# One weight unit's low part on GpSimd, and another order of VectorE's additions and low parts behind the pooled products

## The reference, cut to what matters

```python
x = x + _pool_mixer(h, pool_prev[i], pool_mask, w_pool[i], pool_scale[i])
h = _rmsnorm(x, g_ffn[i])
x = x + _swiglu(h, w1_dense[i // 2], w3_dense[i // 2], w2_dense[i // 2])
# _pool_mixer: y = einsum('btgc,gce->btge', diff, w_pool) * scale
# _rmsnorm:    y = x * rsqrt(mean(x * x) + EPS) * g
# _swiglu:     (silu(h @ w1) * (h @ w3)) @ w2
```

## Time and profile before

| | us |
|---|---|
| median of 3 runs | 1482.81 (1482.11 to 1485.51) |
| the profiled execution's own time | 1484.52 |
| its span in the profile | 1482.7 |
| TensorE busy | 1454.6 (98%) |
| VectorE busy | 1199.4 (81%) |
| ScalarE busy | 1019.6 (69%) |
| GpSimd busy | 35.8 (2%) |

### The profile page before, as it was taken

How to read it: one execution, slowest core, us unless ns; L and a number is a source line. 1 busy time by engine, 2 the same in 40 slices (tenths; PEclk the granted TensorE clock), 3 DMA queues, 4 the chain that set the end, 5 groups by cost and what they waited for, 6 DMA issues and landing times.

```text
span 1482.7 us, 23159 instructions
## 1 busy us (share of the span) xinstructions
PE 1454.6 (98%) x7980; PEld 1278.9 (86%) x7980; DVE 1199.4 (81%) x1441; ACT 1019.6 (69%) x1292; POOL 35.8 (2%) x66
## 2 busy tenths in 40 slices
PE   7999999999999999999999999999999999999997
PEld 7999999999988888888888888888888888888787
DVE  6745545458875899998999999999989999899897
ACT  5433333356786777777877877777787777787776
POOL 2000000000000000000000000000000000000000
PEclk9999999999999999999999999999999999999999
DMA  9434443435413999999999999999999999999951
GB/s 355 175 142 154 144 155 143 152 140 192 164 44 121 359 368 388 381 385 390 360 387 381 352 410 373 363 403 379 373 391 379 385 375 381 388 361 399 378 198 36
DMA packets 65827, 437.69 MB, mean 295 GB/s; under 512 B 8643, under 2 KB 10307, under 8 KB 14704
## 3 DMA queue, kind: packets, MB, share of 16 engines
q1 hardware_dynamic: 62592, 426.87, 74.6%
q0 software_dynamic: 2768, 9.89, 2.6%
q10 hardware_dynamic: 416, 0.26, 0.1%
HBM read 428.22 MB, written 8.77 MB: 295 GB/s over the span
## 4 chain that ended last, share of the span: by engine, by line
PE 93%; DVE 4%; ACT 1%; DMA 1%; issue 1%; SPq 0%; DVEq 0%; ACTq 0%; POOLq 0%
PE PS L742 90%; PE PS L1158 2%; DMA s_G<-in_x_rows 1%; PE PS L1114 0%; DVE s_Al L1254 0%; DVE s_Sl L1241 0%; DMA s_G<-rows_dram,s_ix 0%; DVE s_xT L1320 0%; ACT s_hT L452 0%; DVE s_st L1495 0%; ACT s_Sh L440 0%; PE PS L1064 0%; PE PS L1191 0%; ACT s_sq L452 0%; DVE s_Al L1246 0%
## 5 line engine op out<-in xcount | busy, mean ns | idle before, releaser
L1241 DVE TENSOR_TENSOR s_Sl<-s_raw,s_Sh 128x1024 fp32r<-128x1024 f32 x798 | 937.3, 1221 | 131.2 <-ACT s_Sh L440 130.2
L440 ACT ACTIVATE s_Sh<-s_raw 128x1024 fp32r<-128x1024 f32 x798 | 799.4, 1052 | 215.1 <-PE PS L742 208.5
L742 PE MATMUL PS<-s_Sh,s_Ah 128*128 128x512 f32 x1344 | 529.9, 394 | 0.0
L742 PE MATMUL PS<-s_Sh,s_Al 128*128 128x512 f32 x1344 | 524.1, 390 | 0.0
L742 PE MATMUL PS<-s_Sl,s_Ah 128*128 128x512 f32 x1344 | 523.6, 390 | 0.0
L742 PE MATMUL PS<-s_Ah,s_Sh 128*128 128x320 f32 x1008 | 314.0, 312 | 3.2 <-DVE s_Sl L1241 1.2
L742 PE MATMUL PS<-s_Ah,s_Sl 128*128 128x320 f32 x1008 | 311.8, 309 | 0.0
L742 PE MATMUL PS<-s_Al,s_Sh 128*128 128x320 f32 x1008 | 311.8, 309 | 0.0
L742 PEld LDWEIGHTS PS<-s_Sh,s_Al 128*128 128x128 f32 x1344 | 252.4, 188 | 53.2
L742 PEld LDWEIGHTS PS<-s_Sh,s_Ah 128*128 128x128 f32 x1344 | 252.7, 188 | 50.8
L742 PEld LDWEIGHTS PS<-s_Sl,s_Ah 128*128 128x128 f32 x1344 | 252.9, 188 | 50.6
(11 more groups left out here) (216 smaller groups left out, 586.1 us busy)
## 6 DMA issues: line engine op xcount, KB each, us to landing
s_raw<-in_w_moe SPq DMA_DIRECT2D x336, 1024.0 KB, 6.5
s_raw<-in_w_trunk SPq DMA_DIRECT2D x63, 1024.0 KB, 4.8
y_dram<-s_G POOLq DMA_DIRECT2D x3, 512.0 KB, 4.0
s_xT<-in_xT SPq DMA_DIRECT2D x2, 640.0 KB, 15.3
s_G<-in_x_rows SPq DMA_DIRECT2D x2, 512.0 KB, 5.6
rows_dram<-s_G SPq DMA_DIRECT2D x4, 256.0 KB, 2.0
s_G<-y_dram SPq DMA_DIRECT2D x2, 512.0 KB, 7.5
out_y<-s_G SPq DMA_DIRECT2D x2, 512.0 KB, 3.0
```

Of the source, the lines that this page charges most:

```text
L440: nc.scalar.activation(Sh[:, q % NSPL, o:o + UNIT // 2], raw[:, q % NRAW, o:o + UNIT // 2], ACT.Copy).then_inc(hi_ready, 1)
L742: return nc.tensor.matmul(out, w, m, start=start, stop=stop, **kw)
L1241: last = nc.vector.tensor_tensor(Sl[:, q % NSPL, o:o + UNIT // 2], raw[:, q % NRAW, o:o + UNIT // 2], Sh[:, q % NSPL, o:o + UNIT // 2].bit ...
```

## The change

GpSimd makes the low part of unit 2, behind unit 1's, in the same two halves; VectorE no longer does. VectorE adds chunks 0 and 1 ahead of `lo(1)`, makes the low parts of chunks 0 and 1 behind it, then adds chunks 2 and 3 and makes theirs. `lo(3)` moves from behind the sum tree to ahead of it, behind a wait for the third low part. ScalarE makes the high part of unit 3 between chunks 3 and 4 in place of behind the squares, and the squares follow the last high part. TensorE's and SP's streams are not changed.

```diff
--- before.py
+++ after.py
@@ -381,6 +381,12 @@
             pool.wait_ge(hrows_ready, 3)
             pool.dma_start(A["pool_prompt"], hrows[P - HIST:P, 1, :]).then_inc(pool_stored, 16)
             pool.dma_start(A["pool_sample"], hrows[TS - HIST:TS, 2, :]).then_inc(pool_stored, 16)
+            pool.wait_ge(lo_ready, 2)
+            for half in range(2):
+                o = half * (UNIT // 2)
+                pool.wait_ge(hi_ready, 5 + half)
+                last = pool.tensor_tensor(Sl[:, 2, o:o + UNIT // 2], raw[:, 2, o:o + UNIT // 2], Sh[:, 2, o:o + UNIT // 2].bitcast(F32), ALU.subtract)
+            last.then_inc(lo_ready, 1)
             pool.wait_ge(unit_done, Q_PROJ + 1)
             pool.memset(xrow, 0.0).then_inc(consts, 1)
             pool.wait_ge(consts, NCONST + 2)
@@ -486,11 +492,12 @@
                 act.wait_ge(band_done, c + 1)
                 nc.scalar.activation(Ah3[:, c, :], PS[:, c, 0:T], ACT.Copy).then_inc(hh_ready, 1)
             hi(1)
+            act.wait_ge(vec_loaded, 16)
             hi(2)
-            act.wait_ge(vec_loaded, 16)
-            high_g(1, G_FFN0, 1)
+            high_g(1, G_FFN0, 1, 0, 4)
+            hi(3)
+            high_g(1, G_FFN0, 1, 4, KC)
             squares(1, 0, KC)
-            hi(3)
             root(1)
 
             def silu(r, b):
@@ -1304,13 +1311,15 @@
             for c in range(KC):
                 v.wait_ge(hh_ready, c + 1)
                 low(Al3[:, c, :], PS[:, c, 0:T], Ah3[:, c, :], hl_ready)
-            lo(1)
             v.wait_ge(vec_loaded, 16)
             for c in range(KC):
+                if c == 2:
+                    lo(1)
+                    low_g(1, G_FFN0, 0)
+                    low_g(1, G_FFN0, 1)
                 if c == 4:
-                    for d in range(4):
-                        low_g(1, G_FFN0, d)
-                    lo(2)
+                    low_g(1, G_FFN0, 2)
+                    low_g(1, G_FFN0, 3)
                 if c % 4 == 0:
                     v.wait_ge(x_loaded[c // 4], 16)
                 if c < KC - 1:
@@ -1322,8 +1331,9 @@
                 if c > 4:
                     low_g(1, G_FFN0, c - 1)
             low_g(1, G_FFN0, KC - 1)
+            v.wait_ge(lo_ready, 3)
+            lo(3)
             tree(1)
-            lo(3)
             norm(1)
             link(nc.vector.memset(rsc[:, :], 1.0))
             v.wait_ge(consts, 4)
```

## The result

| | us | runs |
|---|---|---|
| before, on the same chips | 1483.14 (1481.68 to 1486.20) | 22 |
| the change | 1486.58 (1484.05 to 1490.35) | 22 |
| ratio | 1.0024, 95% interval 1.0018 to 1.0030 | |
| the profiled execution of the change | 1485.56 (span 1483.8) | 1 |

The change is slower, by 3.4 us between the medians. That is 0.24% (0.18 to 0.30), just above the 0.2% (3.0 us) that the prediction set as the smallest difference to be told from none, and inside its range.

What follows compares the result with a forecast made beforehand. TensorE, busy 98% of the span, was taken to bound the kernel. Chunk 2 3.72 us late, less 1.24 us gained at unit 3, gave 2.5 us slower: 1485.3 us, range 1481.1 to 1487.4.

Steps and rivals of the forecast that it cites:

- The forecast's mechanism: GpSimd's two halves each hold a VectorE activation low part, so TensorE starts chunk 2 3.72 us late; chance 0.40.
- C: Rival: VectorE held twice and TensorE's clock falls in the waits; 3.7 us slower, 1486.5 us, chance 0.13.
- the likeliest, without the fall: Forecast case: VectorE's low parts held twice, TensorE's clock unchanged; 2.5 us slower, 1485.3 us, chance 0.40.
- The fall: TensorE's granted clock dropping to 1.2 GHz around its waits before chunk 2; at most 1.7 us, put at 1.2.
- The wait for unit 3: TensorE's idle time behind the sum of squares, for weight unit 3's low part; 1.24 us, expected to go entirely.
- A, no hold: Rival: GpSimd's and VectorE's subtractions run side by side, only 1.24 us gained; 1481.6 us, chance 0.25.
- B, held once: Rival: VectorE's first two low parts both go between GpSimd's halves; 0.9 us slower, 1483.7 us, chance 0.22.
- The places where I had found cover: TensorE reaches the square sum at 45.0, ready near 44; unit 3's scaled gate has 0.7 us of cover.
- no change: Outcome for the whole kernel: a difference of under 0.2% (3.0 us) from before; chance 0.67.

Runs made afterwards that it cites:

- e4: The change with GpSimd's low part of unit 2 in four instructions of 512 columns instead of two of 1024; 1484.26 us, ratio 1.0003.
- e6: The kernel before with only GpSimd's making of unit 2's low part added; 1484.01 us, ratio 1.0004.
- e7: The change with GpSimd's two subtractions replaced by four fills of nearly the same total length; 1481.94 us, ratio 0.9987.
- e8: The change with GpSimd also waiting until the low parts of chunks 0 and 1 are made; 1485.32 us, ratio 1.0013.
- e3: The change with 18 small filler products added on TensorE where it waits ahead of the first three chunks; 1485.04 us, ratio 1.0011.
- e1: The change without GpSimd: VectorE makes unit 2's low part behind four activation low parts; 1482.44 us, ratio 0.9994.
- e2: The kernel before with only unit 3's high and low parts moved to their new places; 1481.52 us, ratio 0.9989.
- e5: The kernel before with unit 3's new place and VectorE adding chunks 0 and 1 ahead of unit 1's low part, no GpSimd; 1481.46 us, ratio 0.9982.

## Why the prediction was right, and where it was off

**The forecast's mechanism is shown, step by step.** From the end of the pooled low parts I had put GpSimd's start at 3.28 us (25.15 - 21.87), the end of the first low part at 5.88, of the second at 8.48, TensorE's chunk 2 at 10.68. They came at 3.27, 5.97, 8.54 and 10.70 (23.81, 26.51, 29.08 and 31.24, less 20.54). Chunk 2 is 3.69 us late where I had 3.72; before, it starts at 28.88 and not at my 28.83:

```profile
28.88 0.31 PE L742 MATMUL PS<-s_Ah,s_Sh 128*128 128x320 f32 x1
```

That the steps fit to 0.1 us is luck in part. GpSimd's subtraction was taken at 2.04 us for 1024 columns from rows of 3 and 24; it releases VectorE 2.15 us after its start (if the low part's work is 0.55) and is shown with 2.36, and a quarter with 1.29, so the slope is (2.36 - 1.29) / 512, 2.1 ns a column. The 2.25 us estimated from the Trainium skill (GPSIMD Engine Reference, as in the prediction) is as near to the 2.15. Its rule of the shared port (SBUF — State Buffer, section Who interferes with whom) had been shown by no row for this pair; e4, e6, e7 and e8 now agree with it: two SBUF inputs are held, one SBUF input and PSUM are not, and a GpSimd fill does not hold two SBUF inputs.

**What was off is the weight of a rival.** The case that came is C: both holds and a fall of the clock. I gave it 0.13, and the likeliest, without the fall, 0.40. The fall was priced at 1.2 us. In the trace the nine product intervals from 31.24 to 33.76 take 2.52 us instead of 9 x 0.148 = 1.33, 1.2 lost, and e3 gets 1.1 back. I had held against C that 1.04 us of idle time had left the clock alone. But the change makes that wait 1.97 us and puts one of 0.71 behind it, and the clock had fallen by 27 us, as behind the 1.53 in the earlier trace rows. It is not one profile's accident: the mean granted clock is 0.9961 over the change's 22 runs and 0.9963 in e8, against 0.9974 over 33 of before and 0.9973 to 0.9976 in all other experiments. 0.0013 of 1484 us is 1.9 us of clock missing in the mean, part of it spent in waits. The profiled execution misses 3.4 us in the stretch (6.8 us at 0.50), so the mean run loses less there, or less elsewhere; which of the two is open.

What decides on a fall stays open as well. The length of one wait alone does not: the clock fell behind 1.53 us of idle time (before near 480 us, and e3 and e7 ahead of the stretch) and 1.79 (e1), and did not behind 1.58 (e4), 1.55 and 1.37 (e6) and 1.59 (the change, before 482.06). Apart from the change's, every one of these profiles has a fall of 3.4 us near 480, so falls that the change has no part in come and go between executions.

**One term was mis-sized.** The wait for unit 3 was counted with its 1.24 us of idle time behind the record of the sum (to 41.98). The next product can start 0.30 us behind the sum's start, so the wait is worth 1.64 (e2: 1.6). Another 0.08 us is gained where TensorE takes up unit 2 (the next product follows in 0.15 us, before in 0.23), probably because the unit is ready sooner. The sum is then 3.69 + 1.19 - 1.64 - 0.08 = 3.2 us, as by distance, and 3.4 between the medians. My 2.5 for the likeliest case would have been 2.0. The 0.4 too little for this wait and the 1.2 of the fall that I left out pull opposite ways, and so the forecast missed by less than the fall alone would have made it.

**The rivals that fell.** A, no hold: the two long low parts refute it, and e7 shows its time. B, held once: the second low part is not served with the first, it waits for GpSimd's second half in the change, e3 and e6, and e4's pair of low parts is parted by a quarter. The places where I had found cover held: no wait for the square sum, and the scaled gate, ready at 58.47, is 13.4 us behind unit 3's start at 45.06, within the two units that follow.

The prediction's time, 1485.3, is 1.3 below the measured one; of the chances, most (0.67) lay on "no change", up to 0.2%, and the measured 0.24% (0.18 to 0.30) is at that border, on the slower side.

## What to carry to other kernels

Before work is moved to GpSimd, look at what VectorE runs beside it: if GpSimd's instruction reads SBUF and VectorE's reads two SBUF tensors, the later one waits until the other's instruction is through, so a 0.55 us step can cost 2.6. Short GpSimd instructions cost less (e4), and fills cost such a step nothing (e7). Price a wait that is added ahead of TensorE with the clock as well: behind waits of 1.97 and 0.71 us another 1.2 us was lost here. And try each part of a change alone: here the new place of unit 3 gained 1.6 us and the rest lost 4.8, and the part that gains, with another order of additions, beats both kernels (e5).

## What was not expected of the hardware

- With both engines queued, VectorE's waiting instruction was served between two of GpSimd's, and then GpSimd's before VectorE's next, although VectorE's instructions otherwise overlap by 0.09 us (two in 1.01 us). That is also the order of their starts in the profile (GpSimd's second at 26.14, VectorE's second at 26.44), so whether they alternate or are served in the order of asking is not separated.
- GpSimd seems to release VectorE before its own record ends: with 0.55 us for its work VectorE starts it at 25.96, and the record ends at 23.81 + 2.36 = 26.17, 0.2 us later. The same working gives 0.2 us for e4's first quarter and for e8's first half.
- The granted clock can fall to 1.2 GHz behind idle times of 1.97, 1.53 or 1.43 us and stay there while TensorE works: 6.8 us in the change (5.95 of them at work), 2.8 us from 31.01 in e8. Other executions kept 1.00 behind 1.55 to 1.59 us.
